# Gate rows of a pooling and mLSTM layer issued between the first pool steps, with their scratch in other buffers

## What is computed

```python
h = rmsnorm(x, g_norm) * (1 + scale) + shift          # shift, scale, gate from c
u = h @ w_in                                          # 7176 columns
xp, zp, q, k, v, o, zm, ig, fg = split(u)
y_pool = pool_mixer(xp, ...) * silu(zp)               # 4 groups, trailing windows 2, 4, 8, 16
lf = log_sigmoid(fg + b_f)                            # 4 heads, one number per token and head
F = cumsum(lf);  a = (ig + b_i) - F;  m = F + max(m0, cummax(a))
# chunked recurrence per head with weights exp(a + F_L - m_L), decays exp(m0 + F_L - m_L)
hm = head_layernorm(num / max(|nq|, exp(-m))) * g_head
y_m = hm * sigmoid(o) * silu(zm)
y = rmsnorm(x + gate * (concat(y_pool, y_m) @ w_out)) # outputs: y, pool rows, C, n, m
```

## Time and profile before

| what | value |
|---|---|
| median of the runs, slowest core | 2308.23 us |
| the profiled execution's own time | 2314.72 us |
| its span on the slowest core, core 5 | 2313.3 us |
| spans of the 8 cores | 2294.3 to 2313.3 us |
| TensorE, VectorE, ScalarE, GpSimd busy | 66%, 47%, 30%, 14% of the span |
| granted clock, mean of core 5 | 0.854 |
| table loads of ScalarE | 83, 1.28 us each |

### The profile page before, as it was taken

How to read it: one execution, slowest core, us unless ns; L and a number is a source line. 1 busy time by engine, 2 the same in 40 slices (tenths; PEclk the granted TensorE clock), 3 DMA queues, 4 the chain that set the end, 5 groups by cost and what they waited for, 6 DMA issues and landing times.

```text
span 2313.3 us, 28236 instructions; the slowest of 8 cores (2294.3 to 2313.3 us)
## 1 busy us (share of the span) xinstructions
PE 1538.4 (66%) x8592; PEld 851.8 (37%) x8592; DVE 1078.0 (47%) x2782; ACT 693.7 (30%) x1253; POOL 335.3 (14%) x420
## 2 busy tenths in 40 slices
PE   2228786776697876838778777669787674764443
PEld 2215343433353433414444343335343341353331
DVE  0004554565536556525455556553655652622233
ACT  0252232333622322316233233352232232011120
POOL 2021212221101112101011122110111210000000
PEclk9998998987988988969799899898998896866665
DMA  9646355064502132154310110450213315437958
GB/s 140 132 82 112 55 107 91 10 137 148 181 37 11 60 51 15 64 114 146 109 45 21 46 55 19 150 179 36 11 59 51 19 59 96 131 98 92 105 63 73
DMA packets 96781, 185.66 MB, mean 80 GB/s; under 512 B 17736, under 2 KB 76720, under 8 KB 89592
## 3 DMA queue, kind: packets, MB, share of 16 engines
q1 hardware_dynamic: 46728, 158.15, 30.8%
q0 software_dynamic: 49904, 25.71, 9.6%
HBM read 166.68 MB, written 42.86 MB: 91 GB/s over the span
## 4 chain that ended last, share of the span: by engine, by line
PE 37%; DVE 21%; ACT 13%; issue 11%; DMA 9%; POOL 5%; SPq 3%; DVEq 1%; ACTq 0%; POOLq 0%
PE ps L166 35%; ACT sb_hT L174 5%; DVE sb_Call L188 3%; ACT sb_xhatn L174 3%; DMA sb_xsn<-x 3%; DVE sb_yo L178 3%; SPq L200 2%; ACT sb_Cbf L174 2%; PE ps L170 2%; DVE sb_ycatT L188 2%; POOL sb_yv L178 2%; POOL sb_stt L178 2%; DVE sb_hn L184 2%; DMA sb_hslot<-w_ada 1%; DMA sb_hslot<-w_in 1%
## 5 line engine op out<-in xcount | busy, mean ns | idle before, releaser
L166 PE MATMUL ps<-sb_hT,sb_hslot 128*128 128x512 bf16 (+1 forms) x2304 | 503.9, 377 | 2.3 <-issue 1.4
L166 PEld LDWEIGHTS ps<-sb_hT,sb_hslot 128*128 128x128 bf16 x2304 | 226.8, 104 | 247.2 <-issue 33.0
L166 PE MATMUL ps<-sb_hT,sb_pslot 128*128 128x512 bf16 (+1 forms) x1152 | 265.9, 395 | 0.0
L166 PE MATMUL ps<-sb_vaug,sb_PT 128*128 128x257 bf16 (+1 forms) x144 | 42.2, 293 | 274.1 <-DVE sb_hn L184 165.9
L178 POOL TENSOR_TENSOR sb_stt<-sb_stt,sb_mhalf 128x1 f32<-128x1 f32 (+1 forms) x144 | 78.8, 547 | 859.7 <-DVE sb_stt L188 720.2
L174 ACT ACT_TABLE_LOAD x83 | 106.5, 1283 | 289.1 <-PE ps L166 279.1
L188 DVE SCALAR_TENSOR_TENSOR sb_ycatT<-ps,sb_vecT,sb_gm 128x128 bf16<-128x128 bf16 (+1 forms) x288 | 97.7, 339 | 179.0 <-PE ps L170 140.6
L174 ACT ACTIVATE sb_Cbf<-sb_Call,sb_dLbc 128x257 bf16<-128x257 f32 x272 | 138.9, 511 | 140.0 <-DVE sb_Call L188 112.6
L166 PEld LDWEIGHTS ps<-sb_hT,sb_pslot 128*128 128x128 bf16 x1152 | 118.1, 109 | 131.2 <-issue 33.6
L166 PE MATMUL ps<-sb_hslot,sb_hT 128*128 128x256 bf16 (+1 forms) x1152 | 157.5, 282 | 0.7 <-ACT sb_pstage L174 0.4
L188 DVE SCALAR_TENSOR_TENSOR sb_Call<-sb_Call,sb_dLbc,ps 128x257 f32<-128x257 f32 x272 | 130.1, 478 | 56.1 <-PE ps L166 40.3
(11 more groups left out here) (126 smaller groups left out, 2129.3 us busy)
## 6 DMA issues: line engine op xcount, KB each, us to landing
sb_hslot<-scrH SPq DMA_DIRECT2D x16, 2560.0 KB, 20.9
sb_pslot<-scrP SPq DMA_DIRECT2D x24, 1024.0 KB, 8.1
sb_xsn<-x SPq DMA_DIRECT2D x33, 512.0 KB, 5.0
sb_xpT<-x SPq DMA_DIRECT2D x33, 512.0 KB
y<-sb_yo SPq DMA_DIRECT2D x33, 512.0 KB, 3.2
sb_hslot<-w_in POOLq DMA_DIRECT2D x20, 512.0 KB, 21.3
scrH<-sb_hslot SPq DMA_DIRECT2D x4, 2560.0 KB, 8.9
sb_hslot<-scrH SPq DMA_DIRECT2D x4, 2048.0 KB, 19.2
```

Source lines behind the costliest of these rows:

```text
L166: return lambda e: e.matmul(out, lhsT=lhsT, rhs=rhs, start=start, stop=stop)
```

## The change

The gate stage is no longer written as a whole ahead of the steps. `gate_phase` and `gatebc_phase` become generators that yield at nine points (one of them once for each half of the tokens), `steps_gen` yields after every piece of the steps, and `interleave` takes one piece of each in turn, steps first. Before the first dependent part of a head, whatever is left of the gate chain is written out. The scratch moves: rb_ to xsn0, rsp to xsn1 (the norm stage's input tiles), rN to feature rows 14 and 15 of ycatT read as fp32, under a new name of its own; the first scan into rN also counts as a write of all of ycatT. The early exits on `stop` go.

```diff
-            rb_ = yv[0][0:4, 0:n]; r_rb = r_yv[0]
-            rsp = yo[0][0:4, 0:n]; r_rsp = r_yo[0]
+            rb_ = xsn[0][0:4, 0:n]; r_rb = r_xsn[0]
+            rsp = xsn[1][0:4, 0:n]; r_rsp = r_xsn[1]
             rGn = gate_bc[0:4, 0:n]; r_rGn = r_gbc
-            rN = xs[0][0:4, 0:n]; r_rN = r_xs[0]
+            rN = ycatT[:, 14:16, :].rearrange("p a b -> p (a b)").bitcast(F32)[0:4, 0:n]; r_rN = r_rowN
...
                 fw.op("act", ACT(rsp[:, cs], bk[0:4, 0:N], AF.Exp, scale=-1.0, bias=sm4[0:4, 2:3]), reads=[rb, r_bias], writes=[r_rsp])
+                yield
             fw.op("act", ACT(rsp, rsp, AF.Ln, bias=1.0), reads=[r_rsp], writes=[r_rsp])
...
             fw.op("dve", TT(rb_, rb_, rGn, ALU.add), reads=[r_rb, r_rGn], writes=[r_rb])
+            yield
...
-                      reads=[r_rb, r_carry, r_m0T], writes=[r_rN])
+                      reads=[r_rb, r_carry, r_m0T], writes=[r_rN] + (list(r_yc) if si == 0 else []))
+            yield
...
             fw.op("act", ACT(rfl, rfl, AF.Exp, scale=2.0), reads=[r_rGn], writes=[r_rGn])
+            yield
...
+        def chain2(a, b):
+            for _ in a:
+                yield
+            for _ in b:
+                yield
+
+        def steps_gen(mb, ntg, gate_chain):
...
+            k0, i0, t0_ = steps[0]
+            for _ in INP[k0](mb, i0, t0_, ntg):
+                yield
+            gate_done = False
+            for si_, (kind, i, tg) in enumerate(steps):
+                nxt = steps[si_ + 1] if si_ + 1 < len(steps) else None
+                if kind == "H" and not gate_done:
+                    run_all(gate_chain)
+                    gate_done = True
+                gen_dep = DEP[kind](mb, i, tg, ntg)
+                gen_in = INP[nxt[0]](mb, nxt[1], nxt[2], ntg) if nxt is not None else None
+                for _ in interleave_gen(gen_dep, gen_in, 1, 2):
+                    yield
...
-            gate_phase(mb)
-            gatebc_phase(mb)
...
+            gate_chain = chain2(gate_phase(mb), gatebc_phase(mb))
+            interleave(steps_gen(mb, ntg, gate_chain), gate_chain, 1, 1)
```

More of the change, by code:

```diff
@@ L708, in build @@
         ccount = [0]
+        r_rowN = R("rowN")
         r_C2 = [R("C2_%d" % i) for i in range(4)]
@@ L910, in build, with interleave_gen @@
         prev_final = None
+        def interleave_gen(a, b, ra=1, rb_=1):
+            gens = [a, b]
+            rates = [ra, rb_]
+            alive = [a is not None, b is not None]
+            while any(alive):
+                for gi in range(2):
+                    if not alive[gi]:
+                        continue
+                    for _ in range(rates[gi]):
+                        try:
+                            next(gens[gi])
+                        except StopIteration:
+                            alive[gi] = False
+                            break
+                yield
+        def chain2(a, b):
+            for _ in a:
+                yield
+            for _ in b:
+                yield
+        def steps_gen(mb, ntg, gate_chain):
+            steps = []
+            for i in range(4):
+                for tg in range(ntg):
+                    steps.append(("P", i, tg))
+                for tg in range(ntg):
+                    steps.append(("H", i, tg))
+            k0, i0, t0_ = steps[0]
+            for _ in INP[k0](mb, i0, t0_, ntg):
+                yield
+            gate_done = False
[7 more added lines that the diff above has]
+                for _ in interleave_gen(gen_dep, gen_in, 1, 2):
+                    yield
+                if tg == ntg - 1:
+                    if kind == "P":
+                        if i + 2 < 4:
+                            load_pool_w(i + 2)
+                        elif i == 3:
+                            load_wout_a()
+                    else:
+                        if i + 2 < 4:
+                            load_head_w(i + 2)
+                        elif i == 2:
+                            load_wout_b()
         for mi, mb in enumerate(mbs):
@@ L918, in build @@
             load_head_w(0)
-            if stop < 1:
-                continue
-            gate_phase(mb)
-            gatebc_phase(mb)
[L923 to L930, removed]
-            steps = [st_ for st_ in steps if stop >= 3 + (st_[1] * 2 + (1 if st_[0] == "H" else 0))]
-            if steps:
-                k0, i0, t0_ = steps[0]
-                run_all(INP[k0](mb, i0, t0_, ntg))
-            for si_, (kind, i, tg) in enumerate(steps):
-                nxt = steps[si_ + 1] if si_ + 1 < len(steps) else None
-                gen_dep = DEP[kind](mb, i, tg, ntg)
-                gen_in = INP[nxt[0]](mb, nxt[1], nxt[2], ntg) if nxt is not None else None
-                interleave(gen_dep, gen_in, 1, 2)
-                if tg == ntg - 1:
-                    if kind == "P":
-                        if i + 2 < 4:
-                            load_pool_w(i + 2)
-                        elif i == 3 and stop >= 11:
-                            load_wout_a()
-                    else:
-                        if i + 2 < 4:
-                            load_head_w(i + 2)
-                        elif i == 2 and stop >= 11:
-                            load_wout_b()
+            gate_chain = chain2(gate_phase(mb), gatebc_phase(mb))
+            interleave(steps_gen(mb, ntg, gate_chain), gate_chain, 1, 1)
             flush(pend_hn)
             flush(pend_tr)
-            if stop < 11:
-                continue
             prev_final = final_phase(mb)
```

## The result

The changed kernel takes 2341.12 us in the median against 2311.63 of the kernel before beside it: ratio 1.013, 95% interval 1.0106 to 1.0153, some 30 us slower where 66 were forecast. In some executions the cores of a die show a lower granted clock; these stand in the two medians but in no ratio here (without them the medians are 2336.0 and 2308.2), and where a comparison had too few others, I read the cores whose clock was not lowered, and call them undisturbed.

What follows compares the result with a forecast made beforehand. No engine was taken as full; time is set stage by stage. Block costs of 7, 15.4, 16.6, 15.4 and 12 us gave about +66 on the median 2308.23: 2374 us, range 2336 to 2396.

Steps and rivals of the forecast that it cites:

- a: Block 2's gate stage: TensorE waits for pslot0 in front of everything, gate products included, 12.5 us.
- b: Block 2's gate stage: the first 8 products of P0 restart a dropped clock, 3.4 us.
- c: Block 2's gate stage: 32 gate and 8 more P0 products at full speed, 9.0 us.
- d: Block 2's gate chain up to Xd, lengthened by foreign ScalarE and VectorE work: 24.6 us, TensorE standing 13.8 of it.
- e: Block 2, after Xd: fp32 products at dropped clock, 16.1 us, plus four wpool products, 1.7: 17.8 us.
- f: Block 2, the head's first products: one more restart at half clock, 1.6 us.
- the rival in which it stays up: Prompt blocks' fp32 products: bf16 products beside them keep the clock at 1.00, saving 8 us each; 2342 us, chance 0.08.
- the chain was lengthened: Gate chain: forecast lengthening; the rival had foreign work falling into idle time, +19 us, 2327 us, chance 0.10.
- the cover: Rival for the gate stages: P0's products fill the gap with no weight wait, 47 us faster, 2261 us, chance 0.04.
- the relocated scratch costs nothing: Gate rows' new scratch places: same shapes and engines, buffers free there, so no cost by itself.
- All terms are differences inside it, so they go on the median: Whole kernel: +66 us from the profiled execution's span added to the median 2308.23, giving 2374 us.
- the last rival: Gate chain slips further, one more load and ACTIVATE at four joins in four blocks: +30, 2404 us, chance 0.04.

Runs made afterwards that it cites:

- e4: Changed kernel with both halves of the gate products written ahead of P0's first product, the rest interleaved: gates sum 274 us, undisturbed cores 2297.9 to 2300.7 us.
- e5: Changed kernel with the gate chain whole up to the exp of the rows, then interleaved: cores at clock 0.86 span 2264 to 2271 us; no ratio formed.
- e1: Changed kernel with the gate stage written whole ahead of the steps again in all blocks, only the scratch moved: undisturbed cores 2294.8 to 2300.8 us.
- n1: Kernel before without its 48 small stores of n, otherwise unchanged: undisturbed cores 2200 to 2221 us.
- n4: Kernel before, complete, with n stored as one 1-KB row for each sequence and head: undisturbed cores 2208 to 2217 us.
- n3: Kernel before changed to write the gate chain first up to its rows' exp, then interleave with P0, and store n as rows: 2205.29 us, ratio 0.9586.

## Why the prediction was wrong

**Right, term by term.** Block 2 on core 7, forecast and then measured from the timeline above: a, wait for pslot0, 12.5 and 11.9; b, first 8 products, 3.4 and 3.5; c, 9.0 and 8.9 (642.16 to 651.09); d, from there to Xd, 24.6 and 25.5, with 13.8 and 14.98 of it idle; e and f together, 19.4 and 18.1 (676.60 to the head's first product at 694.70). The sum is 68.9 against 68.0. The clock was at 0.50 through the fp32 products, which refutes the rival in which it stays up; the chain was lengthened, and the cover did not work, as e4 and e5 show from the other side. The gates of blocks 1 to 5 were to cost 7, 15.4, 16.6, 15.4 and 12 and cost 8.3, 14.4, 16.7, 15.3 and 7.8: 63 of 66. Only block 5's was off by more than 1.5 us; it cost 6.4 to 10.1 by core. The sentence that the relocated scratch costs nothing holds by e1, and the table loads are 104 for 105.

**Wrong, one step.** "All terms are differences inside it, so they go on the median", and with it the silent assumption that all that lies outside the gate stages keeps its time. 46 us of it did not in the profiled executions (some 39 against the other programs with a long stall, the end included, which brings 63 and the steps' few us to the 30 measured). So the step that failed is a term put at nothing without a reason: the waits for transfers behind the small stores of n, in the norm stages behind blocks 2 and 4 and in the rest of block 5. g2, which is the change without its fourth table set, runs at 1.0304, which on 2308.23 is 2378 us; the forecast of 2374.0 was a forecast of that kernel. The range ended at 2336 for the same reason: its bounds came from the terms of the gates, and none from the transfers elsewhere. That 2341.12 still lies inside it is luck, and so is its nearness to the 2342 of the rival in which the clock stays up: the clock did not. The forecast put 0.80 on a change of more than 2%, and it came out at 1.3%. That 0.80 was also added wrong: the forecast's 0.74 and the last rival's 0.04 make 0.78 at most, and what stays within 2% had at least 0.18.

Could it have been seen? The stall, yes: the wait of 16.34 us for x behind block 2 and the landing of 25.8 us stood in the trace of before. There was also a rule that I did not weigh. The Trainium skill (DMA: Bandwidth & Descriptors, Specifications) says that a transfer under 512 B is done as a read-modify-write; the runs agree that the 4-byte stores are what costs, with C's 1-KB packets left in place (n1, the 90 or 76 to 82 us above), though none shows a read-modify-write. The switch, no: that a fourth table set would bring the stall from 15 to 9 us no row tells, and the order of the instructions alone does not tell that block 1 brings one. But the number of table sets can be read from the compiled program.

The rule of the Trainium skill on table loads that was weighed (ScalarE: Activation LUTs, What ACT_TABLE_LOAD costs: a drain of about 1380 ns with every switch) is not borne out here either: 657.35 plus 1.28 is 658.63, and the Silu starts at 658.64.

## What to carry to other kernels

Before a change is priced, list the transfers that come in packets of a few bytes and read how long the first load behind them takes; here one fp32 product per store and a copy for every two, which turn two columns into a row, were worth more than any reordering (some 75 us of span alone in n4, 0.96 together with the order in n3). When a profile differs at places whose instructions didn't change, look at what the two compiled programs differ in, not only at the order: take the suspect alone, in both directions, and beside it an edit of the same size that lacks the suspect, which is missing here. And fill a gap in a chain only with work that is issued behind the whole chain on every engine of it, and whose own inputs have landed.

## What the runs showed that I had not expected

- Two small edits on ScalarE, by the compiled programs one that adds a table set and one that takes it away, change what the small stores cost: 0.984 when added, 1.030 against 1.013 when taken away. Found by elimination; the way of working is open.
- Neighbouring cores seem to share what the 4-byte stores need. With three table sets the stall is 14.1 us in the mean (10 to 17) where they store within 2 us, 9.8 (8 to 12) where they are over 6 us apart. The distance is taken from each core's own trace, which starts at its first instruction, so it is rough.
- The stall shows on the first packets behind the stores, not on the stores' own records: in block 2 the packets of n_o are recorded with some 9 ns each, and the load behind them carries the 15 us. In the view of DMAs the price appears under hslot, in the waits under x, and n_o shows nothing.
